# A 31-tap convolution branch: first tap on ScalarE, two float32 weight units, conditioning sums spread, idle products in the opening

## The reference, cut to what matters

```python
mod = silu(c) @ w_ada + b_ada            # conditioning: 6 x 1024 numbers
sh1, sc1, g1, sh2, sc2, g2 = split(mod, 6)
h = layer_norm(x) * (1 + sc1) + sh1
a_val, a_gate, u_pool, gate_a, gate_b = split(h @ w_in)
ya = causal_dwconv(a_val * sigmoid(a_gate), w_dw_a) + b_dw_a   # 31 taps, 512 channels
ya = silu(layer_norm(ya, ln_a_g, ln_a_b)) @ w_pw_a             # 512 -> 1024
pooled = windowed means of u_pool over 2, 4, 8, 16 tokens - u_pool
yb = (pooled @ w_pool per group) * pool_scale
mix = (sigmoid(gate_a) * ya + sigmoid(gate_b) * yb) @ w_out    # 1024 -> 1024
x = layer_norm(ALPHA * x + g1 * mix, ln1_g, ln1_b)
```

## Time and profile before

| | |
|---|---|
| median of 3 runs | 1041.59 us (1041.11 to 1041.85) |
| the profiled execution's own time | 1043.17 us |
| its span | 1041.4 us |
| mean granted clock of TensorE | 0.996 of full |
| busy: PE, DVE, ACT, POOL | 98%, 73%, 55%, 3% |
| weights and other reads | 198.71 MB |

### The profile page before, as it was taken

How to read it: one execution, slowest core, us unless ns; L and a number is a source line. 1 busy time by engine, 2 the same in 40 slices (tenths; PEclk the granted TensorE clock), 3 DMA queues, 4 the chain that set the end, 5 groups by cost and what they waited for, 6 DMA issues and landing times.

```text
span 1041.4 us, 18360 instructions
## 1 busy us (share of the span) xinstructions
PE 1020.8 (98%) x7497; PEld 956.5 (92%) x7497; DVE 761.0 (73%) x1314; ACT 577.8 (55%) x967; POOL 27.4 (3%) x32
## 2 busy tenths in 40 slices
PE   7999899999999999999999999999999999999997
PEld 7999898999999998999987999999899878999996
DVE  7999898799877788877867555555889676555555
ACT  6564447766555586724646544544746565445443
POOL 0000000000100042000000000000000000000000
PEclk9999999999999999999999999999999999999999
DMA  9999764587756533622345555666364426655611
GB/s 372 419 418 384 256 229 176 184 271 271 241 186 193 173 101 111 224 73 67 97 142 179 167 183 192 190 190 191 117 232 161 126 98 245 216 185 183 185 58 41
DMA packets 59603, 201.22 MB, mean 193 GB/s; under 512 B 10496, under 2 KB 10880, under 8 KB 59264
## 3 DMA queue, kind: packets, MB, share of 16 engines
q1 hardware_dynamic: 58368, 199.98, 56.5%
q10 hardware_dynamic: 1152, 0.07, 0.1%
HBM read 198.71 MB, written 1.31 MB: 192 GB/s over the span
## 4 chain that ended last, share of the span: by engine, by line
PE 83%; DVE 12%; ACT 3%; issue 1%; DMA 1%; SPq 0%; ACTq 0%; DVEq 0%
PE ps L622 72%; PE ps L994 4%; DVE lo L1882 2%; DVE raw L1869 1%; DVE B L2337 1%; PE ps L709 1%; ACT hi L1282 1%; PE ps L800 1%; DVE B L1955 1%; PE ps L851 1%; DMA raw<-in_w 1%; PE ps L788 0%; DMA B<-in_t 0%; DVE sm L2161 0%; PE ps L1218 0%
## 5 line engine op out<-in xcount | busy, mean ns | idle before, releaser
L1882 DVE TENSOR_TENSOR lo<-raw,hi 128x1024 fp32r<-128x1024 f32 x300 | 364.7, 1222 | 118.4 <-ACT hi L1282 117.8
L622 PE MATMUL ps<-hh,hi 128*128 128x256 f32 x1544 | 437.7, 284 | 5.2 <-DVE hl L1928 2.7
L622 PE MATMUL ps<-hl,hi 128*128 128x256 f32 x1544 | 432.8, 280 | 0.0
L622 PE MATMUL ps<-hh,lo 128*128 128x256 f32 x1544 | 432.4, 280 | 0.0
L1282 ACT ACTIVATE hi<-raw 128x1024 fp32r<-128x1024 f32 x308 | 322.2, 1052 | 53.5 <-PE ps L622 50.1
L622 PEld LDWEIGHTS ps<-hh,hi 128*128 128x128 f32 x1544 | 291.7, 189 | 9.5 <-issue 3.8
L622 PEld LDWEIGHTS ps<-hl,hi 128*128 128x128 f32 x1544 | 291.8, 189 | 1.8 <-issue 0.3
L622 PEld LDWEIGHTS ps<-hh,lo 128*128 128x128 f32 x1544 | 291.8, 189 | 0.0
L622 PE MATMUL ps<-hi,fh 128*128 128x512 f32 x192 | 76.3, 397 | 0.0
L622 PE MATMUL ps<-lo,fh 128*128 128x512 f32 x192 | 75.9, 395 | 0.0
L622 PE MATMUL ps<-hi,fl 128*128 128x512 f32 x192 | 75.8, 395 | 0.0
(11 more groups left out here) (333 smaller groups left out, 1257.5 us busy)
## 6 DMA issues: line engine op xcount, KB each, us to landing
raw<-in_w SPq DMA_DIRECT2D x359, 512.0 KB, 4.4
Z<-in_w SPq DMA_DIRECT2D x7, 512.0 KB, 9.5
B<-in_t SPq DMA_DIRECT2D x2, 512.0 KB, 4.6
xa<-in_x SPq DMA_DIRECT2D x1, 1024.0 KB, 12.0
B<-in_w SPq DMA_DIRECT2D x2, 512.0 KB, 8.1
h<-in_w SPq DMA_DIRECT2D x2, 512.0 KB, 8.3
B<-in_r SPq DMA_DIRECT2D x1, 1024.0 KB, 7.1
out<-h SPq DMA_DIRECT2D x4, 256.0 KB, 2.0
```

The lines of the kernel that those rows point to most:

```text
L622: m = g.matmul(o, l, r, start=first and n == 0, stop=last and n == 2, skip_group_check=True)
L1882: g.tensor_tensor(lo[:, j % SPLIT, :], raw[:, PLACE[j] % RAW, :], hi[:, j % SPLIT, :].bitcast(F), ALU.subtract).then_inc(*up("lo", j))
```

## The change

1. **First tap on ScalarE.** `tap(0)` leaves VectorE's list; ScalarE writes it (`tap0`) as four instructions between its own copies of the odd and even channels and the sigmoid of gate 4.
2. **Pooling.** The windows are summed over fixed columns, since 16 zero columns ahead of each buffer (two more memsets on GpSimd) make the copies needless. The edge means of all four groups take three instructions in place of eight.
3. **Two units in full float32.** `pw0` and `out0` are no longer split and leave PLAN; they come through the `cw` slots as units 11 and 12, and `rows_plain` multiplies them with the unsplit `cv` and `mg`: 8 products of full float32 each in place of 24. Their high and low parts, and those of input part 0, are gone. Every call `UNIT[x] + AHEAD` ahead of them now names a unit one place further on.
4. **Conditioning rows spread.** Two of the late `ada` calls go into the last two rounds, one ahead of the statistics, the others between the low parts of `pw`, where the `low` calls for the coming units now stand too.
5. **Idle products.** 6 and 18 in the opening after the transposes, 18 in place of 10 ahead of the norm, and the 6 ahead of `pw0` gone.
6. **Norm all on VectorE.** Both channel halves are normed there (L2025 four times), the two ScalarE instructions (L1384) and the small one for their bias (L2022) are gone.

```diff
+ROWS_PLAIN = [("pw", 0), ("out", 0)]
...
-CW_AFTER = {u: m for m, u in enumerate([("in", n) for n in range(22, 28)] + [("pw", n) for n in range(4)] + [("out", 0)])}
+CW_AFTER = {u: m for m, u in enumerate([("in", n) for n in range(22, 28)] + [("pw", n) for n in (1, 2, 3)]
+                                        + [("ada", n) for n in (28, 31, 33)] + [("out", 1)])}
...
+                spin(18 if c else 6, 3)
...
             s.wait_ge(*at("yb", 7))
-            spin(10)
+            spin(18)
...
-            spin(6, 5)
-            for k in range(4):
-                rows_in("pw", k, 2, yh[:, k, :], yl[:, k, :], at("silu_lo", k), k == 0, k == 3,
+            def rows_plain(i, b0, x):
+                m = len(SHIFTS) + i
+                s.wait_ge(s_cw[m % CW_SLOTS], 16 * (m // CW_SLOTS + 1))
+                for n in range(8):
+                    g.matmul(acc(b0, n), cw[m % CW_SLOTS][:, n * P:n * P + P], x, start=n % 2 == 0, stop=False, skip_group_check=True)
+
+            s.wait_ge(*at("silu_y", 0))
+            rows_plain(0, 2, cv[:, 0, :])
+            for k in range(1, 4):
+                rows_in("pw", k, 2, yh[:, k, :], yl[:, k, :], at("silu_lo", k), False, k == 3)
+            s.wait_ge(*at("silu_y", 3))
+            s.wait_ge(*at("merged", 0))
+            rows_plain(1, 6, mg[:, 0, :])
...
+                    for t in range(4):
+                        g.activation(cv[:, t, :], ypad[:, t, 2:2 + S], ACT.Identity, scale=V("w_dw_a", t * 31),
+                                     bias=V("b_dw_a", t)).then_inc(*up("tap0", t))
...
                 if k == 1:
-                    high(UNIT["pw", 0] + AHEAD)
-            for k in range(1, 4):
+                    high(UNIT["pw", 1] + AHEAD)
+            for k in range(2, 4):
                 high(UNIT["pw", k] + AHEAD)
...
                 if n < TAPS_V - 4:
                     tap(4 + n)
+                elif n > 5:
+                    ada(late + n - 6)
...
+            ada(late + 2)
             for b in range(2):
                 s.wait_ge(*at("ya_tok", b))
...
-            for n in range(3):
-                ada(late + n)
-            for k in range(4):
+            for k in range(1, 4):
                 s.wait_ge(*at("silu_y", k))
                 s.wait_ge(*at("silu_hi", k))
                 g.tensor_tensor(yl[:, k, :], cv[:, k, :], yh[:, k, :].bitcast(F), ALU.subtract).then_inc(*up("silu_lo", k))
-                if k % 2:
-                    ada(late + 3 + k // 2)
-            for k in range(3):
-                low(UNIT["pw", k] + AHEAD)
+                if k < 3:
+                    low(UNIT["pw", k] + AHEAD)
+                ada(late + 2 + k)
```

More of the change, by code:

```diff
@@ L116, in stream_plan @@
             plan += [("ada", i // 2), ("ada", 8 + i // 2)]
-        plan.append(u)
+        if u not in ROWS_PLAIN:
+            plan.append(u)
         n = ROWS_AT.get(i, 1 if i >= 52 and i % 3 == 0 else 0)
@@ L583, in gpsimd @@
             g.memset(up_pad[:, :, 0:16], 0.0).then_inc(*up("fill", "pool"))
+            for i in range(2):
+                g.memset(win[i][:, :, 0:16], 0.0).then_inc(*up("fill", ("win", i)))
             g.memset(y_even[:, :, 0:16], 0.0).then_inc(*up("fill", "even"))
@@ L756, in tensor @@
             s.wait_ge(*at("gate_b", 7))
-            spin(6, 5)
-            for k in range(4):
-                rows_in("pw", k, 2, yh[:, k, :], yl[:, k, :], at("silu_lo", k), k == 0, k == 3,
[L760 to L763, removed]
+            def rows_plain(i, b0, x):
[10 more added lines that the diff above has]
+            rows_plain(1, 6, mg[:, 0, :])
+            for k in range(1, 8):
+                rows_in("out", k, 6, hh[:, k, :], hl[:, k, :], at("merged_lo", k), False, k == 7)
             def turn_in(nid, made, between=None):
@@ L1381, in scalar @@
             table(ACT.Silu)
[L1382 to L1385, removed]
             for k in range(4):
@@ L1400, in scalar @@
             for k in range(8):
-                high(UNIT["out", k] + AHEAD)
+                if k:
+                    high(UNIT["out", k] + AHEAD)
                 scale_x(k)
@@ L1985, in pool_group @@
                                     ALU.subtract).then_inc(*up("pooled", q - 1))
+            late = PLACE[UNIT["pw", 3]] + 1
             for n in range(4):
                 window(n)
-                tap(n)
+                if n:
+                    tap(n)
                 low(UNIT["in", 16 + n] + AHEAD)
@@ L1994, in vector @@
                 low(UNIT["in", 20 + n] + AHEAD)
+                if n == 0:
+                    pool_edges()
                 if n < 2:
@@ L2008, in vector @@
             g.tensor_tensor(yb[:, 7, :], yb[:, 7, :], ev[:, 3, :], ALU.mult).then_inc(*up("ybg", 7))
-            late = PLACE[UNIT["pw", 3]] + 1
+            ada(late + 2)
             for b in range(2):
@@ L2021, in vector @@
             s.wait_ge(*at("trs", "ya"))
-            g.scalar_tensor_tensor(out=fnm, in0=fmv[:, :, 0:1], scalar=-1.0, in1=frs, op0=ALU.mult,
-                                   op1=ALU.mult).then_inc(*up("tnm", "ya"))
-            for v in range(2):
-                g.tensor_scalar(yt[:, v, 0:S], bank[0][:, v * S:v * S + S], fmv[:, v, 0:1], frs[:, v, :], ALU.subtract,
-                                ALU.mult).then_inc(*up("norm_v", ("ya", v)))
-            for n in range(3):
-                ada(late + n)
-            for k in range(4):
+            for b in range(2):
+                for v in range(2):
+                    g.tensor_scalar(yt[:, v, b * S:b * S + S], bank[b][:, v * S:v * S + S], fmv[:, v, 0:1], frs[:, v, :],
+                                    ALU.subtract, ALU.mult).then_inc(*up("norm_v", ("ya", b, v)))
+            for k in range(1, 4):
                 s.wait_ge(*at("silu_y", k))
@@ L2052, in vector @@
             merged_low(7)
-            for k in range(5):
+            for k in range(1, 5):
                 low(UNIT["out", k] + AHEAD)
@@ L2719, in _weights @@
     }
-    return np.stack([units[k][n] for k, n in PLAN] + _shifts(g["w_dw_a"][0]))
+    return np.stack([units[k][n] for k, n in PLAN] + _shifts(g["w_dw_a"][0]) + [units[k][n] for k, n in ROWS_PLAIN])
 def _shifts(w):
```

48 lines of the change are left out of this document (23 added, 25 removed).

## The result

| | before | changed |
|---|---|---|
| median | 1041.59 us (5 runs, 1040.87 to 1042.71) | 1046.77 us (5 runs, 1044.90 to 1046.84) |
| profiled execution, span | 1043.17, 1041.4 | 1044.90, 1043.1 |

The ratio of the two is 1.0037, with a 95% interval of 1.0026 to 1.0048: slower by 0.37%, beyond the 0.2% that can be told. The two medians as they stand are 5.2 us apart, which would be 0.50%; I go by the ratio. The five executions of the changed kernel stand in two groups, 1044.9 and 1045.2 at a granted clock of 0.997, and 1046.8 three times at 0.995. The profile is of the lower group.

What follows compares the result with a forecast made beforehand. TensorE, busy 1020.8 of 1041.4 us, was the bound. `pw0` start -1.0, float32 +0.64, clock +0.1, wait +2.5, `out` +0.3, next norm -0.25 gave +2.3 on 1041.59: 1043.9 us, range 1040.2 to 1045.6.

Steps and rivals of the forecast that it cites:

- The start of `pw0`: Behind the norm of ya: `pw0` starts at 127.2 against 128.16, 1.0 us gained.
- wait at `pw3`: TensorE waits 2.5 us ahead of `pw3` for `silu_lo` 3, behind high part, low part and two sums on VectorE.
- `pw0` in float32: Eight full float32 products take 3.44 us against 2.80 for a split unit, 0.64 longer.
- `out` ends: End of `out` on TensorE at 166.4, 2.6 us later than before.
- the fall that I put at `pw0`: TensorE's clock falls again after the lull from 123.4 to 127.2, at a full price of 1.6 us.
- This wait hangs on `pw1`'s end and not on when the stage begins: At `pw3`: an earlier norm does not remove the 2.5 us wait; without the two sums it would be 0.2.
- The sums ahead of the statistics: VectorE's sums ahead of the norm of ya delay the statistics from 120.61 to 122.7, 2.1 us later.
- The table load: ScalarE's load ahead of silu 0 takes 1.28 us without a drain; with a drain `pw0` would start 1 us later.
- clock +0.1: At `pw0`: a fall costing 1.6 us replaces the earlier one costing 1.5, net +0.1.
- the rival of 1045.5: The clock falls once more, in the 2.5 us wait ahead of `pw3`, costing 1.5 to 1.6 us; chance 0.17.
- These edits cancel: Before round 2: opening, tap 0 on ScalarE and pooling leave TensorE and VectorE within 0.3 us of where they were.
- the opening's gain: With the clock held by 18 idle products, `ina1` starts at 21.2 instead of 21.91, 0.7 us earlier.

Runs made afterwards that it cites:

- e1: The changed kernel with `silu_lo` 3 placed ahead of `low` of `out3` and two `ada` sums on VectorE; ratio to before 0.9996, median 1042.83 us.
- e3: The changed kernel with 18 idle products on TensorE in the wait at `pw3`; ratio to before 1.0020, median 1044.44 us.
- e10: The changed kernel with tap 0 back on VectorE; ratio to before 1.0027, median 1045.95 us.
- e12: e3 with 30 idle products in place of 18 ahead of the turn at the norm; ratio to before 1.0012, median 1044.10 us.
- e2: e1 with ada28, ada29 and ada30 behind the norm instead of ahead of the statistics; ratio to before 0.9974, median 1040.60 us.
- e11: The kernel before with 18 idle products instead of 10 ahead of the turn and 18 instead of 6 ahead of `pw0`; ratio 1.0000, median 1042.11 us.
- e5: e2 with tap 0 back on VectorE; ratio to before 0.9970, median 1039.63 us.
- e8: e2 with the pooling as before, its short copies and separate edge means restored; ratio to before 0.9981, median 1040.31 us.
- e7: e2 with `pw0` and `out0` split in high and low parts again; ratio to before 1.0011, median 1043.92 us.
- e4: The kernel before with only the 6 and 18 idle products in the opening; ratio to before 0.9988, median 1041.32 us.
- e9: e5 with one `ada` sum, ada33, moved from ahead of the merge to behind its last low part; ratio to before 1.0033, median 1046.02 us.

## Why the prediction was right, and where it was not

**Right: slower, and why.** The start of `pw0` gained, and the wait at `pw3` took more than it gave. The steps stand beside the rows:

| step | predicted | profiled execution |
|---|---|---|
| `ina1` | 21.2 | 21.02 |
| first shift | 68.6 to 68.8 | 68.61 |
| statistics | 122.7 | 122.24 |
| norm | 125.1 to 126.9 | 124.53 to 126.4 |
| `pw0` starts | 127.2 | 126.76 |
| `pw0` in float32 | 3.44 + 1.6 for a fall | 3.30, no fall |
| wait at `pw3` | 2.5 | 2.39 |
| `pw3` after the wait | 2.80 | 4.43, a fall of 1.63 |
| `out` ends | 166.4 | 165.90 |
| span against before | +2.3 | +1.7 |

For the profiled execution the sum came out near by luck: the fall that I put at `pw0` (1.6) didn't come, and one that my sum left to a rival came behind the wait (1.63). e1 shows the wait's worth with the fall behind it, 4.3 us; e3's 1.7 for the fall's share is not clear of the noise. "This wait hangs on `pw1`'s end and not on when the stage begins" held: in e10 the norm is 0.83 us sooner and the wait 2.40. The sums ahead of the statistics hold up the norm as was said: 1.63 us later than before, where I had 2.1, and 1.46 us are won when three of the four stand behind it (e2).

The table load took what the row of before has: it ends at 125.6 in the changed kernel, and the next instruction follows at once. The Trainium skill (ScalarE: Activation LUTs, What ACT_TABLE_LOAD costs) counts a drain with every switch of table, and no trace here shows it.

**The term that was mis-sized: the clock.** I wrote "clock +0.1", one fall before and one after, and gave the second fall "in the 2.5 us wait" 0.17. In the profiled execution it is this one that happened, and three of five executions are 1.9 us longer still at 0.995. e10 spells out the levels of nearly the same program: 1042.7 at 0.999, 1044.2 and 1044.3 at 0.997, 1045.9 to 1046.5 at 0.995. So the usual execution most likely falls twice, which is one fall more than the forecast has, as in the rival of 1045.5; e12, where no execution falls, is lower by 2.6 us, beyond both intervals. 1.0037 times 1041.59 is 1045.4, inside my range by 0.2; the measured median itself, 1046.8, lies 1.2 us above its upper end. In the traces of the changed kernels the clock fell behind gaps of 1.74 (e1) and 2.39 us, and it did not behind 1.64 (the changed kernel), 1.65 (e3) and 2.40 (e10). The Trainium skill's rule (TensorE: Matmul & The Clock Gate, HAM oscillation), bursts between waits that start at half clock, is what I had weighed too lightly; the trace agrees where the clock fell, and the three gaps without a fall show that it doesn't happen each time.

**The base.** I laid a difference of profiled executions on the median of others, and assumed the falls of before to be in it. e11 took away the fall at `pw0`, in the profiled execution at least, and gained nothing that can be told. Beside the experiments the kernel before has the lower clocks, 0.991 to 0.997, so its executions seem to fall at least as often as the changed kernel's. How many falls its median holds, and so how much of the 3.9 us is the clock's, stays open.

**Two steps were right in the sum and wrong in the parts.** "These edits cancel": tap 0 on ScalarE moves all later places by 1.0 us in e2's surroundings (e5) and by 0.8 in the changed kernel's (e10), and TensorE's slack at the norm doesn't absorb it, because VectorE's full list from 95 us starts with a wait for a high part (0.45 us in all three traces), and that follows TensorE's pace. The low part stands at 93.91 us in e10, at 94.75 in the changed kernel and at 95.13 before; it was the opening's gain, not the pooling edits (e8: nothing), that paid for it. One reading under this step was wrong: the first shift of before didn't wait for ScalarE's copies, which end at 67.33, but for its own weights (TensorE's weight loads before):

```profile
67.80 1.30 PEld L709 LDWEIGHTS ps<-Z 128*128 128x128 f32 x11 [0.23 <-DMA Z<-in_w]
```

And float32 was charged with +0.64 as a loss. For TensorE alone it is one, 0.50 (3.30 for 2.80), but e7 shows that splitting the two units ends `out` 2.0 us later in e2's surroundings, and costs 3.3 to 3.9 us of time, as the chains of high and low parts come back ahead of both.

**What stays open.** The spread of up to 2.5 us at one clock (e12). One source was caught, the small instruction that takes 0.16 us in e4 and 2.4 in all other traces; that it also parts e2's 1038.9, e5's 1038.0 and e12's 1042.3 from the rest of their runs would fit and is not shown. Nor is it known why that instruction has two lengths, or why e11 and e12 lose 0.9 and 0.7 us behind the root. Both issue more idle products; whether those cost time elsewhere wasn't tried.

**A version that beats both.** e5 keeps edits 2, 3, 5 and 6, has tap 0 on VectorE and the sums behind the norm and behind `silu_lo` 3: 1039.63 us, ratio 0.9970 (0.9959 to 0.9981), 0.3% faster than before (0.2% by the medians on its chip) and, ratio against ratio, 0.67% faster than the changed kernel.

## What to carry to other kernels

Where a wait is filled or moved, price the clock behind it as a term of its own, and read the granted clock of all executions, not only that of the profiled one: here a wait of 2.39 us cost 4.0 in the profiled execution, with the fall of 1.63 behind it. When filler work is spread over an in-order engine, look at what each piece now stands ahead of (here the last low part) and also at which buffer it frees: one sum that ended 11 us later stopped the whole stream of loads (e9). And an engine with slack at a meeting point may still set the pace of the engine that has none, through what it hands over earlier.

## What the runs showed of the hardware

The clock falls in the same gap of the same code in some executions and not in others: behind a wait of 2.39 us it fell in the changed kernel's profiled execution, behind one of 2.40 in e10's it didn't, and the gaps at the norm are followed by 0.86 before and by 1.00 in e4. In the traces a fall cost 1.3 (e1) to 1.6 us (changed), and the levels of executions lie 1.5 to 1.9 us apart. With idle products in both gaps the clock stayed up in all twelve executions of e12. The stream of weights runs at 411 to 422 GB/s with its engines at a share of 1.01 to 1.03 until about 95 us; the weights of the first shift land at 67.7 to 68.1 whatever TensorE has gained (e4, e5, e9, e10, e11). A unit of eight float32 products of 256 columns took 3.26 to 3.35 us at full clock, 1.18 times the split unit's 2.80 for the usual 3.30. A VectorE instruction of 128x16 took 0.16 us in one execution and 2.41 to 2.43 in 13 others.
